# Sixteen routed experts: 64 seats each, rounded rows and rests side by side in one stationary operand

## The reference, cut to what matters

```python
def grouped_moe(x, w_router, b_router, w_gate, w_up, w_down):
    scores = jax.nn.softmax((xt @ w_router + b_router), axis=-1)      
    grp = scores.reshape(-1, 4, 4)
    g_sel = jnp.argmax(jnp.sum(lax.top_k(grp, 2)[0], axis=-1), axis=-1)
    ...
    top_w, top_i = lax.top_k(in_grp, 2)
    top_w = top_w / jnp.sum(top_w, axis=-1, keepdims=True)
    ...
    for e in range(16):
        h = jax.nn.silu(xt @ w_gate[e]) * (xt @ w_up[e])
        y = y + gate[:, e:e + 1] * (h @ w_down[e])
```

## Time and profile before

| | |
|---|---|
| median of three runs | 2308.36 us |
| span of the profiled execution (first to last instruction) | 2304.4 us |
| TensorE matmuls busy | 2264.1 us, 98% |
| VectorE busy | 1599.8 us, 69% |
| ScalarE busy | 1243.2 us, 54% |
| read from HBM | 487.40 MB |
| experts' stage, layer 0 | about 1488 to 1786 us |
| experts' stage, layer 1 | about 1992 to 2293 us |

### The profile page before, as it was taken

One profiled execution on the slowest core, in us unless ns is written; L12 is line 12 of the kernel. 1 busy time (PEld: TensorE's weight loads), 2 busy tenths in 40 slices (PEclk: granted clock), 3 DMA queues, 4 the chain that ended last, 5 costly groups with the idle time before them and its releaser, 6 DMA issues.

```text
span 2304.4 us, 31674 instructions
## 1 busy us (share of the span) xinstructions
PE 2264.1 (98%) x13500; PEld 1969.0 (85%) x13500; DVE 1599.8 (69%) x1552; ACT 1243.2 (54%) x1272; POOL 48.1 (2%) x67
## 2 busy tenths in 40 slices
PE   8999999999999999999999999999999999899998
PEld 7888989788888899997888999888888998788886
DVE  6765755777477558556774656688887666688887
ACT  5444644444354346444443545577776545577775
POOL 1000100000000000000000000000000000000000
PEclk9999999999999999999999999999999999899999
DMA  8755453465555554445555554599997554599995
GB/s 249 208 189 176 131 163 126 161 189 187 185 181 183 189 160 143 152 140 171 186 194 190 170 171 165 184 341 346 370 345 277 179 183 148 197 346 345 346 369 186
DMA packets 309953, 490.96 MB, mean 213 GB/s; under 512 B 15504, under 2 KB 205120, under 8 KB 309808
## 3 DMA queue, kind: packets, MB, share of 16 engines
q1 hardware_dynamic: 305712, 475.35, 61.2%
q0 software_dynamic: 3104, 10.38, 1.6%
q10 hardware_dynamic: 992, 3.15, 0.4%
HBM read 487.40 MB, written 1.44 MB: 212 GB/s over the span
## 4 chain that ended last, share of the span: by engine, by line
PE 93%; DVE 4%; ACT 2%; issue 1%; DMA 0%; DVEq 0%; SPq 0%; ACTq 0%
PE PS L687 20%; PE PS L688 20%; PE PS L691 20%; PE PS L764 14%; PE PS L767 7%; PE PS L999 1%; PE PS L964 1%; PE PS L1396 1%; ACT RH L1565 1%; DVE RL L2065 1%; PE PS L938 1%; PE PS L949 1%; DVE X L2450 1%; PE PS L1361 1%; PE PS L1417 1%
## 5 line engine op out<-in xcount | busy, mean ns | idle before, releaser
L2065 DVE TENSOR_TENSOR RL<-RINGS,RH 128x2048 fp32r<-128x2048 f32 x448 | 1017.3, 2273 | 475.9 <-ACT RH L1565 473.4
L1565 ACT ACTIVATE RH<-RINGS 128x2048 fp32r<-128x2048 f32 x447 | 849.0, 1900 | 467.8 <-PE PS L691 449.1
L687 PE MATMUL PS<-RH,HTS 128*128 128x256 f32 (+1 forms) x1696 | 547.0, 334 | 1.0 <-DVE HTS L2756 0.5
L688 PE MATMUL PS<-RH,HTS 128*128 128x256 f32 (+1 forms) x1696 | 536.7, 328 | 0.0
L764 PE MATMUL PS<-HTS,RH 128*128 128x512 f32 x1384 | 415.0, 396 | 1.5 <-DVE HTS L2051 1.3
L691 PE MATMUL PS<-RL,HTS 128*128 128x256 f32 (+1 forms) x1696 | 400.0, 326 | 0.0
L687 PEld LDWEIGHTS PS<-RH,HTS 128*128 128x128 f32 x1696 | 319.3, 188 | 33.4 <-issue 2.5
L688 PEld LDWEIGHTS PS<-RH,HTS 128*128 128x128 f32 x1696 | 320.5, 189 | 28.0
L691 PEld LDWEIGHTS PS<-RL,HTS 128*128 128x128 f32 x1696 | 289.6, 189 | 31.2 <-DVE RL L2065 0.4
L764 PEld LDWEIGHTS PS<-HTS,RH 128*128 128x128 f32 x1384 | 248.0, 188 | 49.4 <-issue 1.7
L767 PE MATMUL PS<-HTS,RL 128*128 128x256 f32 x1408 | 283.2, 281 | 0.1
(11 more groups left out here) (441 smaller groups left out, 2530.5 us busy)
## 6 DMA issues: line engine op xcount, KB each, us to landing
RINGS<-w_in SPq DMA_DIRECT2D x64, 1024.0 KB, 5.3
RINGS<-w_gate SPq DMA_DIRECT2D x64, 1024.0 KB, 5.4
RINGS<-w_up SPq DMA_DIRECT2D x64, 1024.0 KB, 5.5
RINGS<-w_down SPq DMA_DIRECT2D x64, 1024.0 KB, 5.2
RINGS<-ffn_w_up SPq DMA_DIRECT2D x44, 1024.0 KB, 5.3
RINGS<-ffn_w_down SPq DMA_DIRECT2D x44, 1024.0 KB, 4.9
RINGS<-ffn_w_gate SPq DMA_DIRECT2D x43, 1024.0 KB, 5.4
RINGS<-w_out SPq DMA_DIRECT2D x16, 1024.0 KB, 4.9
```

The lines of the kernel that those rows point to most:

```text
L687: mm(dst, a_[0], b_[0], start=start, stop=False)
L688: mm(dst, a_[0], b_[1], start=False, stop=False) if left else mm(dst, a_[1], b_[0], start=False, stop=False)
L1565: A(splits.buffer(RH, RH3)[:, 0:width], RINGS[:, slot, 0:width], ACT.Copy).then_inc(wh_ready, 1)
L2065: TTn(RL[:, slot, 0:width], RINGS[:, slot, 0:width], splits.buffer(RH, RH3)[:, 0:width].bitcast(F32), ALU.subtract).then_inc(wl_ready, 1)
```

## The change

What is changed, all of it in the experts' stage of both layers:

- **64 seats an expert.** Places are counted per group and per expert (`PICK`, 20 columns for each half of the tokens, where `OH` had 4). The tables `SEATX[g]` hold the four experts of a group beside each other, 64 seats each, so that a token has a seat only with the two experts it picked. The other branch is now taken if an expert has more than 64 tokens. `SEATG` keeps the 128 seats of each group, for the way back.
- **Split rows.** ScalarE rounds the rows themselves once a layer (`rows_rounded`, two copies of 128x1024), GpSimd takes their rests (`XL`, two subtractions of 128x1024). `gather` multiplies both by `SEATX[g]`: 32 matmuls of 256 columns. ScalarE and VectorE take the result in four pieces of 512 columns each (two before) and lay out, for each expert, 64 columns of rounded rows beside 64 columns of their rests (`XS`; the sides are swapped for odd experts).
- **One stationary operand for gate and up** (`stacked`). The 128 columns xh | xl are multiplied by wh and by wl: 8 matmuls a slot where there were 12. One half of PSUM's partitions then holds xh·(wh+wl), the other xl·(wh+wl).
- **The fold.** ScalarE copies the half of the rests (64 partitions, `CORG` for gate, `CORU` for up), and one matmul of 512 columns with a swapping table adds it to the other half (`folded`): two copies and two matmuls an expert. Silu and the product with the gate weight then work on 64 partitions.
- **From 64 seats to the group's 128.** In place of the four transposes, four matmuls with `SEL`, made from the tables, transpose and move the rows at once (`selected`). Down, its sum over the group and the scatter stay as they were.
- **Order.** On TensorE the two down slots of e-1 now stand behind up 1 of e, the gather between them, in the last expert of a group. VectorE's multiplication of e-1 stands at the head of expert e, its lead is two slots. SyncE loads in TensorE's new order.
- Routing: comparisons that stood behind `OH` now stand in the gaps before it; some semaphores are shared.

```diff
-                def down(e, first, end, tiles):
-
-                    pe.wait_ge(eh_l, l * NE + e + 1)
-                    add_rows(4, EH, 0, first, False, tiles)
-                    add_rows(4, EH, 2, False, end, tiles)
...
+                def stacked(bank, i, j):
+                    pe.wait_ge(wh_ready, splits.v + splits.n)
+                    wh, wl = (w.rearrange("p (k n) -> p k n", n=DE) for w in (splits.buffer(RH, RH3), RL[:, slot, :]))
+                    for k in range(4):
+                        mm(PS[:, bank, :], XS[:, 4 * i + k, j, :], wh[:, k, :], start=(i + k == 0), stop=False)
+                    pe.wait_ge(wl_ready, splits.v + splits.n)
+                    for k in range(4):
+                        last = mm(PS[:, bank, :], XS[:, 4 * i + k, j, :], wl[:, k, :], start=False, stop=(i == 1 and k == 3))
+                    last.then_inc(chunks_done, 1)
+                def folded(bank, e, rests, count):
+                    pe.wait_ge(rests_copied, 2 * (l * NE + e) + count)
+                    mm(PS[:, bank, :], SWAP[other_rows(e), :], rests[other_rows(e), :], start=False, stop=True, skip_group_check=True).then_inc(fold_ready, 1)
+                def selected(e, bank):
+                    pe.wait_ge(hid_rows, l * NE + e + 1)
+                    for k in range(4):
+                        last = mm(PS[:, bank, k * P:(k + 1) * P], EHID[main_rows(e), 0, k * P:(k + 1) * P], SEL[main_rows(e), e // 2, :], start=True, stop=True)
...
+                        stacked(0, 0, j)
+                        stacked(0, 1, j)
+                        if e:
+                            selected(e - 1, 7)
+                        stacked(2, 0, j)
+                        stacked(2, 1, j)
+                        folded(0, e, CORG, 1)
+                        if e == 0:
+                            seat_tables()
+                        else:
+                            down_part(0, (e - 1) % EG == 0, False, 1)
+                            if j == EG - 1 and g < NG_ - 1:
+                                gather(g + 1)
+                            down_part(1, False, (e - 1) % EG == EG - 1, 1)
+                        folded(2, e, CORU, 2)
...
+                    def hidden(e):
+                        dve.wait_ge(gate_silu, l * NE + e + 1)
+                        dve.wait_ge(fold_ready, 2 * (l * NE + e) + 2)
+                        V.scalar_tensor_tensor(EHID[main_rows(e), 0, :], PS[main_rows(e), 2, :], GSEAT[main_rows(e), e:e + 1], ESIL[main_rows(e), 0, :],
+                                               ALU.mult, ALU.mult).then_inc(hid_rows, 1)
```

More of the change, by code:

```diff
@@ L37 @@
 EG = NE // NG_
+SEATS = 64
 NCMP = 15
@@ L1928, in hidden_rounded, with expert @@
                     A(EH[0][:, :, 0:tiles * P], PS[:, 2:2 + tiles, :].rearrange("p b n -> p (b n)").rearrange("p (k n) -> p k n", k=4), ACT.Copy).then_inc(eh_h, 1)
-                def expert(e, tiles, left=True, more=True, between=None, behind=None):
+                def expert(e, tiles, left=True, more=True):
                     chunk()
@@ L1935, in expert @@
                     split(back=3)
-                    if between is not None:
-                        between()
                     chunk()
@@ L1946, in expert @@
                         chunk()
-                        if behind is not None:
-                            behind()
                         split(back=3)
@@ new lines, in seated @@
+                    def seated(e):
+                        g, j = e // EG, e % EG
+                        chunk()
+                        split(back=3)
+                        chunk()
+                        rests(e, CORG, 0)
+                        split(back=3)
+                        if e:
+                            hidden_copy(e - 1, 7)
+                        chunk()
+                        split(back=3)
+                        chunk()
+                        rests(e, CORU, 2)
+                        act.wait_ge(fold_ready, 2 * (l * NE + e) + 1)
+                        A(ESIL[main_rows(e), 0, :], PS[main_rows(e), 0, :], ACT.Silu).then_inc(gate_silu, 1)
+                        split(back=3)
+                        if e == 0:
+                            seats()
+                            return
+                        chunk()
+                        split(back=3)
+                        if j == EG - 1 and g < NG_ - 1:
+                            gathered(g + 1)
+                        chunk()
+                        if j == 0:
+                            group_rows(g - 1)
+                        if e < NE - 1:
+                            split(back=3)
@@ L1980, in _ @@
                     for e in range(NE):
-                        expert(e, 1, left=e > 0, more=e < NE - 1, between=None if e else seats,
-                               behind=(lambda: group_rows(e // EG - 1)) if e and e % EG == 0 else None)
-                        if e % EG == 1 and e // EG < NG_ - 1:
-                            gathered(e // EG + 1)
-                    hidden_rounded(NE - 1, 1)
+                        seated(e)
+                    hidden_copy(NE - 1, 3)
                     if l == 0:
@@ L2486, in _ @@
                 link(V.memset(STATE[:, 0, :, :], 0.0))
+                if l == 0:
+                    for half in range(2):
+                        link(V.tensor_copy(SWAP[:, half * 64:half * 64 + 64], IDENT[:, 64 - half * 64:P - half * 64]))
                 dve.sem_inc(lv_ready, 1)
@@ L2719, in _, with expert @@
                 apart = steps.n
-                def expert(e, tiles, gate, left=True, more=True, behind=None):
+                def expert(e, tiles, gate, left=True, more=True):
                     if left:
@@ L2763, in _ @@
                     split()
[L2764 removed]
                     if l == 0:
                         split()
[L2767 to L2769 removed]
+                    gathered(0)
                     for e in range(NE):
[L2771 to L2774 removed]
```

363 lines of the change are left out of this document (228 added, 135 removed).

## The result

| | before | changed |
|---|---|---|
| median | 2308.33 us | 2285.57 us |
| runs | 2308.28 to 2308.93 | 2284.42 to 2286.92 |
| span of the profiled execution | 2304.4 us | 2285.1 us |

The ratio is 0.9901, with a 95% interval from 0.9887 to 0.9915. The change gains 22.8 us, 1.0%. Forecast were 44.3 us and a range from 2254 to 2284 us: the direction was right, the size about half, and the time lies 1.6 us above the range.

A forecast was written before the change was run, and what follows sets the result against it. With TensorE relieved, VectorE was to bound: 64.6 us a group, 66.0 with hand-overs and late transfers, for 72.0. Layer gains of 22.8 and 22.9 us, less 0.4 and 1.0, made 44.3: 2264 us, range 2254 to 2284.

The forecast's parts named there:

- The group, 66.0 us: Group of four experts: VectorE's 64.6 us plus 0.6 for hand-overs and 0.8 for late transfers, 66.0 us in place of 72.0.
- TensorE's sum, 60.2 us: TensorE's work in a group: gate and up 29.8, down 22.3, folds 1.9, `selected` 2.4, gather 3.8; 11.8 less than 72.0.
- 8 folds 1.9: TensorE, each group: the eight fold matmuls of 512 columns were to take 1.9 us together.
- 16 matmuls of `selected`, taken like the transposes, 2.4: TensorE, each group: the 16 matmuls that select the seats were to take 2.4 us, as 16 transposes do.
- VectorE's 64.6 us: VectorE's work in a group, 55.0 of it 24 rests at 2.290 us; claimed to set the pace after the change.
- The DMA's 65.4 us at 385 GB/s: Transfers of a group's 24 slots, 25.17 MB: 65.4 us at the rate seen where the queue catches up.
- The case that it sets the pace at 368 GB/s: Rival, experts' groups: the DMA holds a group at 68.4 us, gain 29 us, 2280 us, up to 2295; chance 0.19.
- The start: From routing to each layer's first product: forecast at 1507.0 us in layer 0 and 2014.2 us in layer 1.
- `seat_tables` at 4.7 us: TensorE, ahead of the first product: 16 matmuls of 128 columns, 16 small ones 1.85, eight transposes 1.03; together 4.7 us.
- What follows is the same in both: Behind each layer's last product: the remaining work was to take equally long before and after the change, no loss.
- the chain through the fold takes the place of the bound: Rival, each expert: waits for fold and `EHH` cost VectorE 2 us, 72.6 us a group, 2300 to 2312 us; chance 0.05.
- the clock falls over whole groups: Rival, each group: TensorE's granted clock falls; at 0.75 a group takes 80.3 us, 2375 us in all; chance 0.05.

The follow-up runs named there:

- e3: The changed kernel with one more VectorE operation of 0.69 us an expert (the rest `EHL` written twice): 2287.99 us.
- e11: The e2 kernel with one more VectorE operation of 0.69 us an expert: 2279.37 us.
- e1: The changed kernel with 128 rows instead of 64 for the fold's matmul, its swapping table zero where nothing is wanted: 2278.52 us.
- e2: The e1 kernel with the selection's matmuls on 128 rows too, gate weights zero in the half not wanted: 2276.23 us.
- e6: The changed kernel with down slots halved in loading, rounding and rest, all matmuls kept (output values wrong): 2285.14 us.
- e9: The e2 kernel plus the early seat tables of e4 and ScalarE's silu table loaded ahead of time: 2274.27 us.
- e10: The e9 kernel with gate weights of the seats as rounded part and rest, 16 one-pass matmuls of four columns for 32 entries of two: 2267.22 us.
- e4: The changed kernel with the seat tables' matmuls right behind the first gather, only the eight transposes left ahead of the first product: 2281.93 us.
- e8: The e4 kernel with four entries of 16 columns for the 32 gate-weight matmuls of two columns (gate weights wrong): 2271.43 us.

## Why the prediction went wrong, by its steps

- **The group, 66.0 us: measured 66.1, for another reason.** The step that failed is TensorE's sum, 60.2 us, and with it the wait that was to bound the group: measured are 65.9 us on TensorE, so it and not VectorE sets the pace, and that the total came out was luck. Neither of the forecast's signs of being wrong (a group above 70 us, VectorE under 90% busy; it is 95%) could tell the two apart. Two terms of the sum were mis-sized. "8 folds 1.9" are 8 x 0.62 = 5.0, because a fold was priced as any matmul of 512 columns and its 64 rows were not considered. "16 matmuls of `selected`, taken like the transposes, 2.4" are 4 x 1.27 = 5.1: each is a float32 product with two entries in the trace, not one like a transpose, and has 64 rows too. With 5.8 us more TensorE is the bound. The other sums held: gather 3.8, ScalarE's copies of 64 partitions 0.58 to 0.59 (0.60 taken), the products on 64 partitions 0.75, the folds' copies not on the path.
- **VectorE's 64.6 us were too many by 2.** It is busy for 62.5: rests that follow without a wait start 2.21 us apart, not the 2.29 of one. e3 and e11 show that it has slack.
- **The DMA's 65.4 us at 385 GB/s** came out: e1 and e2 stand at 65.4 to 66.0. It is a mean that fits, not the rate at which the transfers run: that is 394, with a loss behind each gather that the forecast did not have. The case that it sets the pace at 368 GB/s did not come. The Trainium skill's 358 GB/s (page and section as above) did not come either; the rate of 394 in e2 is against it.
- **The start** is the step that cost most, 15.3 of the 25 us. `seat_tables` at 4.7 us with "16 small ones 1.85" compared unlike things: the row of before counts 16 entries, two for each of 8 float32 matmuls, and the change has 16 such matmuls, so 32 entries. It also took full clock for them. The tables take 7.1 us in layer 0 and 9.4 in layer 1, 7.1 more in both together. In layer 0 TensorE also stood for 2.7 us and then ran its first slots at a clock of 0.52, 10.4 us for four slots in place of 7.4. I had priced the low clock once, at 1.0 us. The rest is VectorE's longer routing (2.6 of layer 1's 8.3, where new small operations and a reduction had been priced at nothing) and the fold's 64 rows ahead of the product.
- **First group.** It takes 67.6 and 68.2 us, the later ones 66.1: most of the 2.4 and 3.3 us between first and last product. TensorE is busy in all of it (67.5 and 68.2 us), so next to nothing of it is a wait for the ring, and e6 with fewer bytes has 68.0 and 67.6. By TensorE's folds the first group is 66.8 and 67.3 us, some of it at the low clock that the tables left behind; the rest is that the first product follows its fold by 0.9 us and the later ones by 1.8.
- **The end.** "What follows is the same in both" missed 1.4 and 1.5 us: the last product now comes 0.6 us (layer 1: 0.4) before TensorE is through its twelve scatter matmuls, so these set the time, the selection takes 1.08 us where four transposes took 0.44, and the scatter behind its 64 rows 0.2 more.
- **The rivals.** That the chain through the fold takes the place of the bound was given a chance of 0.05, at VectorE's cost. The fold did cost, but on TensorE itself. That the clock falls over whole groups did not happen, it is 1.00 there; it fell at the starts. The branch for crowded experts was not taken.

## What to carry to other kernels

Price every matmul of an added chain by a row of its own kind, with its rows, type and number of entries: here a matmul of 512 columns with 64 rows among those of 128 cost nearly three times its own time, 0.62 us for 0.23, and with zeros up to 128 rows that was gone. When an engine is relieved of 12 us, write down the next three limits to the same accuracy: here they lay at 66.1 (TensorE), about 65.7 (transfers) and 62.5 us (VectorE), so that removing the first brought next to nothing in the group. A mean rate of transfers over a stretch that another engine holds is no limit; look for the part in which that engine waits. In a stage held by transfers look at its start: the hole in them while the ring was full was not made up in e9, and closing it in e10 gave 7.1 us.

## What was not expected of the hardware

- 0.4 us more for one 64-row matmul among 128-row ones, half of it in its own distance and half in the next (0.42 and 0.43 in place of 0.23 and 0.23), gone with 128 rows (e1).
- A granted clock of 0.50 for 5.2 us behind 32 matmuls of two columns (e4, layer 1) and for 6.0 us from the midst of them on (e9, layer 0), without a gap ahead, and not behind 16 entries of four columns (e10) or four of 16 (e8).
- The same 32 matmuls took between 3.68 and 5.84 us in layer 1 from one profile to the next, with the granted clock; the runs of one such kernel lie up to 7.2 us apart (e2), where those of before lie within 1.7.
- The DMA moves 394 GB/s over 24 us (e2) and 393 over 29 us (e9), and 382 over a whole group, where it showed 368 over 62 us before.
